# Two diffusion-backbone layers with a 16-expert mixture: four gate halves kept aside, and two modulation products moved into the output projection

## The reference

```python
mod = silu(c) @ w_mod[l] + b_mod[l]              # six blocks of 1024: sh1, sc1, g1, sh2, sc2, g2
h   = rms(x, norm1_g) * (1 + sc1) + sh1
x   = x + g1 * (mixers(h @ w_in) @ w_out)        # four parallel mixers
h2  = rms(x, norm2_g) * (1 + sc2) + sh2
aff = softmax(h2 @ router_w)                     # 16 experts
gate, idx = top_k(aff.T, cap)                    # 64 latent and 16 context tokens per expert
y_e = (silu(h2[idx] @ wg_e) * (h2[idx] @ wu_e)) @ wd_e * gate
x   = x + g2 * scatter_add(idx, y_e)             # over all 16 experts
```

## Time and profile before

| | us |
|---|---|
| median of 3 runs | 2039.86 (2038.81 to 2039.9) |
| the profiled execution | 2038.71 |
| its span, first to last instruction | 2036.9 |
| PE busy | 1726.2 (85% of the span) |
| DVE, ACT, POOL busy | 582.2, 518.6, 289.2 |
| HBM read / written | 508.33 MB / 24.41 MB |

### The profile page before, as it was taken

How to read it: one execution, slowest core, us unless ns; L and a number is a source line. 1 busy time by engine, 2 the same in 40 slices (tenths; PEclk the granted TensorE clock), 3 DMA queues, 4 the chain that set the end, 5 groups by cost and what they waited for, 6 DMA issues and landing times.

```text
span 2036.9 us, 65158 instructions
## 1 busy us (share of the span) xinstructions
PE 1726.2 (85%) x29816; PEld 1373.7 (67%) x29816; DVE 582.2 (29%) x971; ACT 518.6 (25%) x1286; POOL 289.2 (14%) x292
## 2 busy tenths in 40 slices
PE   4999889984999888888769968999379998989894
PEld 2555466453999888888735535655279998888884
DVE  2168466242111101011123774742501110101011
ACT  2122366111221212121221315641122121212212
POOL 1166200000000000000011680000000000000001
PEclk7999889986999999999979978999589999999997
DMA  9220911247999999999950228012369999999996
GB/s 391 105 83 0 364 59 43 83 171 256 376 388 392 395 389 400 389 400 390 400 200 1 83 92 329 2 63 93 117 243 381 395 393 388 400 388 399 388 396 257
DMA packets 136647, 533.77 MB, mean 262 GB/s; under 512 B 5888, under 2 KB 6976, under 8 KB 136320
## 3 DMA queue, kind: packets, MB, share of 16 engines
q1 hardware_dynamic: 121616, 482.53, 60.3%
q0 software_dynamic: 6336, 21.63, 4.5%
q10 hardware_dynamic: 8624, 28.61, 3.8%
HBM read 508.33 MB, written 24.41 MB: 262 GB/s over the span
## 4 chain that ended last, share of the span: by engine, by line
PE 44%; DMA 32%; SPq 9%; DVE 7%; issue 4%; ACT 2%; POOL 2%; ACTq 0%; POOLq 0%; DVEq 0%; PEldq 0%; PEld 0%
DMA ring<-in_exp_w_down 16%; PE PS L752 13%; SPq L345 9%; PE PS L672 7%; DMA ring<-in_exp_w_up 5%; PE PS L506 4%; DMA x_rows<-arena 4%; DMA arena<-xn_rows,arena 4%; DMA ring<-in_w_mod 3%; PE PS L565 3%; PE PS L582 2%; PE PS L477 2%; PE PS L478 2%; DVE arena L1201 1%; PE PS L411 1%
## 5 line engine op out<-in xcount | busy, mean ns | idle before, releaser
L752 PE MATMUL PS<-arena,ring 128*64 128x80 f32 x24576 | 898.2, 233 | 97.4 <-DMA ring<-in_exp_w_up 41.6
L752 PEld LDWEIGHTS PS<-arena,ring 128*64 128x64 f32 x24576 | 876.7, 137 | 121.3 <-DMA ring<-in_exp_w_up 48.4
L1039 ACT ACTIVATE arena<-PS,modB,modA 128x64 f32<-128x64 f32 (+1 forms) x544 | 153.5, 421 | 405.6 <-PE PS L738 405.6
L1560 POOL DMA_INDIRECT x_rows<-arena x32 | 45.7, 1429 | 756.6 <-DVE arena L1410 756.6
L672 PE MATMUL PS<-ring,H 128*128 128x512 f32 x320 | 139.2, 593 | 0.0
L1397 DVE TENSOR_TENSOR arena<-arena,PS 128x320 f32<-128x320 f32 x64 | 31.4, 490 | 326.1 <-PE PS L752 326.1
L672 PEld LDWEIGHTS PS<-ring,H 128*128 128x128 f32 x320 | 60.0, 190 | 71.9 <-issue 71.7
L506 PE MATMUL PS<-H,ring 128*128 128x512 f32 x192 | 104.6, 628 | 3.4 <-ACT H L826 3.4
L1051 ACT ACTIVATE arena<-PS 128x320 f32<-128x320 f32 x32 | 14.0, 438 | 346.0 <-PE PS L752 346.0
L1201 DVE SCALAR_TENSOR_TENSOR arena<-arena,par 128x655 f32<-128x655 f32 x72 | 99.0, 1375 | 2.2
L1268 DVE TENSOR_REDUCE stat<-PS 128x2 f32<-128x1280 f32 (+1 forms) x54 | 75.5, 1400 | 62.0 <-PE PS L552 53.5
(11 more groups left out here) (191 smaller groups left out, 1733.9 us busy)
## 6 DMA issues: line engine op xcount, KB each, us to landing
ring<-in_exp_w_down SPq DMA_DIRECT2D x64, 2048.0 KB, 26.5
ring<-in_exp_w_gate SPq DMA_DIRECT2D x64, 2048.0 KB, 24.6
ring<-in_exp_w_up SPq DMA_DIRECT2D x64, 2048.0 KB, 25.0
ring<-in_w_mod SPq DMA_DIRECT2D x24, 2048.0 KB, 18.3
ring<-in_w_in SPq DMA_DIRECT2D x8, 2048.0 KB, 27.6
ring<-in_w_out SPq DMA_DIRECT2D x4, 2048.0 KB, 22.6
arena<-x_rows ACTq DMA_DIRECT2D x15, 512.0 KB, 6.7
x_rows<-arena ACTq DMA_DIRECT2D x10, 512.0 KB, 2.6
```

The lines of the kernel that those rows point to most:

```text
L752: last = mm(PS[r0:r0 + HD, b0 + j // 4, (j % 4) * CAP:(j % 4 + 1) * CAP], halves[:, s, k * 512 + (j % 4) * P + r0:k * 512 + (j % 4) * P + ...
L1039: last = do(xeT[:, jj, c0:c1], PS[:, 6 + part, j * CAP + c0:j * CAP + c1], ACT.Identity, bias=modB[:, 1, v, jj:jj + 1], scale=modA[:, 1, v ...
```

## The change

It does two things in each layer.

1. The first half of the gate matrix of experts 5, 6, 7 and 8 no longer comes through the list at its expert's place. SP fetches the four halves ahead into memory that is idle by then: one into the upper end of `arena` once the convolution's last product is done (`c_pw`), one into `H` once the logits are read (`r_sub`), two into the lower `arena` and the rest of `H` once the residual rows are stored (`x_saved`). In the pass before each of the four experts VectorE copies the half into slot 0 (`unstash`) behind the index copies, and raises `slot_ready[0]` itself. The loops over experts on SP and VectorE become a loop, four written-out passes, and a loop.
2. In layer 0 the two modulation products of layer 1 move from behind L714 into the output projection, in four half products, with PSUM banks 7 and 2 instead of 1 and 2. The release of `w_out`'s slots moves ahead with them, in both layers. ScalarE takes both products ahead of the softmax's exponential.

```diff
+        stash = [[(0, arena[:, 14794:18890])], [(0, Hflat[:, 0:4096])], [(0, arena[:, 0:4096])],
+                 [(0, arena[:, 4096:7168]), (3072, Hflat[:, 4096:5120])]]
...
+        STASHED = (5, 6, 7, 8)
...
-            def expert_load(l, e, order=(0, 1, 2)):
+            def expert_load(l, e, order=(0, 1, 2), stored=None):
...
-                    for h in range(2):
+                    for h in range(0 if m or stored is None else 1, 2):
...
+                sp.wait_ge(c_pw, 2 * l + 2)
+                stash_load(l, 0)
                 expert_load(l, 0, FIRST_EXPERT[l])
+                sp.wait_ge(r_sub, l + 1)
+                stash_load(l, 1)
+                for p in range(2):
+                    sp.wait_ge(x_saved[p], 32 * X_LOADS[p] * (l + 1))
+                stash_load(l, 2)
+                stash_load(l, 3)
...
-                with sp.Fori(0, EXPERTS - 1) as e:
-                    expert_load(l, e + 1)
+                with sp.Fori(1, STASHED[0]) as e:
+                    expert_load(l, e)
+                for i, e in enumerate(STASHED):
+                    expert_load(l, e, stored=i)
+                with sp.Fori(STASHED[-1] + 1, EXPERTS) as e:
+                    expert_load(l, e)
...
+                    if t == LT and l + 1 < LAYERS:
+                        modulate(l + 1, 0, 7, (1,))
                     norm2_turn(l, t)
+                    if t == LT - 1:
+                        pe.wait_ge(o_mm, NT * l + NT)
+                        for s in (wout, wout + 1):
+                            pe.nop().then_inc(slot_used[s], 1)
+                        if l + 1 < LAYERS:
+                            modulate(l + 1, 0, 7, (0,))
+                if l + 1 < LAYERS:
+                    modulate(l + 1, 1, 2, (0,))
                 route(l, LT)
...
+                if l + 1 < LAYERS:
+                    modulate(l + 1, 1, 2, (1,))
+                    pe.wait_ge(mod_taken, MODS_DONE[l + 1, 0])
...
+                if l + 1 < LAYERS:
+                    take_mod(l + 1, 0, next_rows[0], 7)
+                    take_mod(l + 1, 1, next_rows[1], 2)
                 act.wait_ge(r_sub, l + 1)
                 do(logit, logit, ACT.Exp).then_inc(r_exp, 1)
...
+                def unstash(l, i):
+
+                    dve.wait_ge(slot_used[0], FIRST[l][0] + STASHED[i] + CREDIT)
+                    dve.wait_ge(stash_loaded[i], 16 * len(stash[i]) * (l + 1))
+                    for w0, src in stash[i]:
+                        last = V.tensor_copy(halves[:, 0, w0:w0 + src.shape[1]], src)
+                    last.then_inc(slot_ready[0], 16)
...
                     V.tensor_copy(idx_in[0:CAP, :], idxT[0:CAP, bass.ds(e + 1, 1)]).then_inc(e_idx, 1)
+                    if stored is not None:
+                        unstash(l, stored)
```

More of the change, by code:

```diff
@@ L143, in backbone_step_kernel @@
         early_rows = [gated[:, 256 * i:256 * i + 256] for i in range(3)]
-        late_cols = gated[:, 768:784]
+        next_rows = [yb[:, 256 * i:256 * i + 256] for i in range(2)]
+        late_cols = yb[:, 512:528]
+        Hflat = H[:, :, :].rearrange("p k n -> p (k n)")
+        stash = [[(0, arena[:, 14794:18890])], [(0, Hflat[:, 0:4096])], [(0, arena[:, 0:4096])],
+                 [(0, arena[:, 4096:7168]), (3072, Hflat[:, 4096:5120])]]
         fgb = gb1[:, 0, :]
@@ L201, in backbone_step_kernel @@
         e_idx = sem("e_idx")
+        stash_loaded = [sem(f"stash_loaded{i}") for i in range(4)]
         e_gath = sem("e_gath")
@@ L353, in mod_load, with stash_load @@
                 matrix_load(("mod", l, b), ins["w_mod"], l, b * D)
-            def expert_load(l, e, order=(0, 1, 2)):
+            def expert_load(l, e, order=(0, 1, 2), stored=None):
                 for m in order:
                     w = ("exp_w_gate", "exp_w_up", "exp_w_down")[m]
-                    for h in range(2):
+                    for h in range(0 if m or stored is None else 1, 2):
                         slot_load(FIRST[l][m] + e, 2 * m + h, ins[w][l, e, h * 512:(h + 1) * 512, :])
+            def stash_load(l, i):
+                for w0, dst in stash[i]:
+                    n = dst.shape[1] // D
+                    sp.dma_start(dst.rearrange("p (k n) -> p k n", n=D),
+                                 ins["exp_w_gate"][l, STASHED[i], w0 // D * P:(w0 // D + n) * P, :]
+                                 .rearrange("(k p) n -> p k n", p=P)).then_inc(stash_loaded[i], 16)
             mod_load(0, 0)
@@ L402, in finish_phase, with modulate @@
                 pe.wait_ge(phase_done, 4 * (l + 1))
-            def modulate(l, b, bank):
+            def modulate(l, b, bank, parts=(0, 1)):
                 m, rnd = LOADS["mod", l, b]
-                for h in range(2):
+                for h in parts:
                     pe.wait_ge(slot_ready[2 * m + h], 16 * (rnd + 1))
@@ L705, in _ @@
                         route(l, t - 1)
+                    if t == LT and l + 1 < LAYERS:
+                        modulate(l + 1, 0, 7, (1,))
                     norm2_turn(l, t)
+                    if t == LT - 1:
[6 more added lines that the diff above has]
+                    modulate(l + 1, 1, 2, (0,))
                 route(l, LT)
-                pe.wait_ge(o_mm, NT * l + NT)
-                for s in (wout, wout + 1):
-                    pe.nop().then_inc(slot_used[s], 1)
+                if l + 1 < LAYERS:
+                    modulate(l + 1, 1, 2, (1,))
+                    pe.wait_ge(mod_taken, MODS_DONE[l + 1, 0])
                 pe.wait_ge(r_aff, l + 1)
@@ L716, in _ @@
                 turn_mod(l, 5, mod5_rows, 4, 0)
-                if l + 1 < LAYERS:
-                    modulate(l + 1, 0, 1)
-                    modulate(l + 1, 1, 2)
                 pe.wait_ge(gates_picked, 2 * l + 2)
@@ L722, in _ @@
                 if l + 1 < LAYERS:
-                    turn_mod(l + 1, 0, early_rows[1], 4, 1)
+                    turn_mod(l + 1, 0, next_rows[0], 4, 1)
                 for _ in range(LOOP_PAD[l]):
@@ L730, in _ @@
                 if l + 1 < LAYERS:
-                    turn_mod(l + 1, 1, early_rows[2], 5, 0)
+                    turn_mod(l + 1, 1, next_rows[1], 5, 0)
                 finish_phase(l)
@@ L1023, in _ @@
                     wait_apart(act, x_saved[p], 32 * X_LOADS[p] * (l + 1))
-                if l + 1 < LAYERS:
-                    take_mod(l + 1, 0, early_rows[1], 1)
-                    take_mod(l + 1, 1, early_rows[2], 2)
                 save_gates(l, 1, PS[0:16, 0, 0:P])
@@ L1384, in _, with expert @@
                 dve.wait_ge(g_loaded, 64 * (l + 1))
-                def expert(l, e):
+                def unstash(l, i):
[4 more added lines that the diff above has]
+                    last.then_inc(slot_ready[0], 16)
+                def expert(l, e, stored=None):
                     done = l * EXPERTS + e
@@ L1411, in expert @@
                                            ALU.mult, ALU.mult).then_inc(e_y, 1)
-                with dve.Fori(0, EXPERTS) as e:
+                with dve.Fori(0, STASHED[0] - 1) as e:
+                    expert(l, e)
+                for i, e in enumerate(STASHED):
+                    expert(l, e - 1, stored=i)
+                with dve.Fori(STASHED[-1], EXPERTS) as e:
                     expert(l, e)
```

## The result

| | median us | ratio to before, 95% interval |
|---|---|---|
| before (4 runs) | 2039.34 (2037.19 to 2039.9) | |
| the change (4 runs) | 1994.41 (1993.19 to 1996.59) | 0.9787 [0.9775, 0.9799] |
| the change again, later (5 runs) | 1997.53 (1994.15 to 1999.69) | 0.9793 [0.978, 0.9807] |

The change takes 43 us off, 0.0213 x 2039. The first median stands 5.6 us under the forecast and 0.6 us under the lower end of its range, the second 2.5 us under the forecast and inside the range. The profiled execution of the change took 1996.59 us (span 1994.8), the longest of its four, so the traces differ by 42.1 us of span and the medians by 44.9.

The account below looks back on a forecast made before the run. It took TensorE's circle with scatter and gather, then weight transfers, to bound the experts. From the profiled 2038.71, -40.9 for halves and +1.0 for products, copies and fetches at 0, gave 1998.8, about 2000.0 us as median; range 1995 to 2013.

Parts of the forecast that it names:

- The bound: Experts' stages: first the scatter, gather and TensorE circle at 30.0 us per expert, then weight transfers at 33.56 us.
- Four halves leave the queue, -40.9 us: Weight queue amid the experts: each half saves 5.11 us at 410 GB/s, 20.5 us per layer, 40.9 in all.
- The dearer price per half: Weight queue: a half priced at 33.56 / 6 = 5.59 us instead of 5.11, which would give 44.7 us.
- The path keeps all of it: Layer's end: the whole 20.5 us arrives, as engines never idle; the lag can lose 2.3 us more per stored expert.
- Copies at nothing: VectorE at stored experts: each copy takes 2.6 to 3.0 us and hides in its wait for TensorE.
- first rival: Stored experts: the copy holds the gather by 3.7 us, the queue runs dry, 2011.2 us in all; chance 0.12.
- Moved products, +1.0 us: Layer 0's projection: the half products delay the exponential by 1.8 us, partly offset by clock; +1.0, bounds -2.7 and +10.4.
- The bound of -2.7: Layer 0's moved products, lower bound: the two last TensorE steps ahead of the exponential take half their time.
- The fetches, 0 with bounds of 2.8: Ahead of the experts: the four fetches fit into idle DMA time and cost 0; bounds -2.8 and +2.8 us.
- The second rival: Layer 0's projection: half products run at the low clock, 4.0 us each, overrunning by 10.4, to 2009.4 us; chance 0.07.
- the third: Ahead of expert 1's loads: three late fetches delay these by what they save, 2029.6 us; chance 0.05.
- fourth rival: Loops over experts: shifted code makes each of 30 later passes pay a 5.9 us issue wait, 2176 us; chance 0.06.

Follow-up runs that it names:

- Copy later: The change, but VectorE copies each stored half behind the first hidden product instead of right behind the index copies; 0.9781 of before.
- the last four: The change with the halves of experts 12 to 15 kept aside instead of 5 to 8; 0.9856 of before.
- nothing removed: The change with all fetches and copies made, the copies into memory nobody reads, and all halves still through the queue; 0.9987 of before.
- the first four: The change with the halves of experts 1 to 4 kept aside instead of 5 to 8; 0.9886 of before.
- Products only: The change without fetches, copies and cut loops: only the moved products and the early release of `w_out`'s slots; 0.9964 of before.
- the narrow dummies: The change with later copy, layer 0's last two fetches behind the first gather, 64-column dummy products, and 130 and 0 empty instructions, not 0 and 76; 1.0447 of before.
- the wide dummies: The change with later copy, 512-column dummy products around expert 0's start, and 212 and 46 empty instructions left before the loops; 0.9866 of before.

## Why the prediction was right, and where not

- **The bound.** Right. The transfers set the end of each layer, and the first part's slack lets a half leave the queue early and count late. Copy later and the last four show it from both sides.
- **Four halves leave the queue, -40.9 us.** Right: 40.8 by the ratios of the change and nothing removed (uncertain by 3), 39.6 by their traces. The dearer price per half, 44.7 us in all, is not borne out.
- **The path keeps all of it; TensorE's pace up to expert 10, then 33.6 us.** Right, gap by gap. That the lag must not be used up is shown by the first four, where 8.6 us of idle engines cost as much. My limit there came from the lag at expert 1, and at experts 5 to 8 there is enough of it.
- **Copies at nothing, 2.6 to 3.0 us each.** 2.28 us, hidden. L1335's rate was the right neighbour and an upper price.
- **The copy holds the gather (first rival).** The hold is real, 1.05 us per stored expert, and lies under the 2.3 us from which the rival was to decide, so its loss does not come. (By the rival's own terms the hold it feared is 3.6 us and not 3.7.) The Trainium skill (SBUF — State Buffer, section "SBUF: two separate sides") says that the loser of the shared ports blocks until the other instruction is through; the trace agrees, 1.05 us lost for 1.17 us of overlap.
- **Moved products, +1.0 us: wrong in sign.** Products only gained 7.3 us, and its trace has 5.9 of them in layer 0 ahead of expert 0. The half products pay for themselves, because the two last TensorE steps run at 2.4 GHz again: the exponential starts 0.7 us sooner and not 1.8 later. The bound of -2.7 held that case, and I took a value on the other side. The larger part, 4.7 us, is the first gather, which the early release frees from expert 0's loads. I had named the release, but used it only to let the fetches fit.
- **The fetches, 0 with bounds of 2.8: wrong.** With the copies they cost 4.7 us, 3.1 of it beside the first gather of layer 0. I took the gather's price of before (10.10 us, already among loads) as the one that stays, when the products had just made it cheaper. The second rival (products at the low clock) and the third (fetches in front of expert 1's loads) do not occur: those loads start 6.4 us behind the first product (492.68 - 486.31), 7.7 before.
- **The sum.** -40.9 + 1.0 + 0 became -40.8 - 7.3 + 4.7 = -43.4 us. That it meets the 43 measured is no check, since the three are differences in one chain of ratios that ends at the change. The two wrong terms nearly cancel, which is luck; what is left of them, -2.6 us where the forecast had +1.0, with the spread between runs, is why the median stands under the forecast.
- **The loop's code (fourth rival).** It did not occur here: the products' unnamed waits are 9.7 us, 11.7 before. That such waits exist in later passes, and can be worth over 100 us, the narrow dummies show; that the loop's place causes them is not shown.

## What to carry to other kernels

When one queue of transfers sets the end of a stage, price a removed transfer by its bytes at the queue's rate, and then ask at which place the queue still has a lag to spend and later work to spend it on: four halves per layer, with all else alike, gave 43 us amid the experts, 29 at their end and 23 at their start. Two edits that touch the same stretch must be costed together; here one made the first gather 4.7 us cheaper and the other took 3 of that back, so that with the halves in place the products bring nothing that the medians can tell. An empty instruction or a dummy product is not free, and after any change in front of a loop the waits that the profile can't name are worth a look.

## What the runs showed of the hardware that I had not expected

- A SBUF copy of 128 x 4096 fp32 by VectorE (2.28 us) stretched a gather instruction on GpSimd from 0.91 to 1.96 us, and its landing from 7.1 to 8.15 us.
- One indirect gather of 80 rows took 5.16 to 5.30 us with the DMA engines half idle, 8.30 with fetches beside it, 10.10 among expert 0's loads.
- 212 empty instructions on TensorE took 32 us, 0.15 us each. The 38 dummies with 64 columns, 76 matmuls in the trace, took 16.47 us, 217 ns a matmul, and the granted clock stood at 0.50 from 470 to 500 us, although TensorE was shown busy nearly throughout; in the kernel with the wide dummies it was 1.00 from 490 us.
- With the narrow dummies and another count of empty instructions ahead of the loop, the unnamed waits of its products rose from 10 to 120 us, 116 of them in layer 1; the cause stays open.
